# Both mixers of the first block worked out between the projection units, and two banks for the modulation rows

## The reference, cut to what matters

```python
def hybrid_mixer(h, positions, w_in, w_alpha, b_alpha, gla_g, gn_g, gn_b, w_out):
    proj = (h @ w_in).astype(F32)                      # 256 tokens, 1024 -> 3600
    gq, gk, gv, gr, ga, rq, rk, rv, rg = jnp.split(proj, np.cumsum(IN_SPLITS)[:-1], axis=-1)
    log_a = jax.nn.log_sigmoid(ga @ w_alpha + b_alpha) / GLA_TAU
    o_g = gla_core(...)                                # 4 heads, chunks of 64, states passed on
    o_g = o_g * lax.rsqrt(jnp.mean(o_g * o_g, axis=-1, keepdims=True) + EPS)
    o_g = o_g.reshape(bsz, seq, GLA_V) * gla_g * jax.nn.silu(gr)
    rq, rk = rotary(rq) * RET_DK ** -0.5, rotary(rk)
    o_r = retention_core(rq, rk, rv, log_gamma)        # 4 heads, chunks of 64
    mu = jnp.mean(o_r, axis=-1, keepdims=True)
    var = jnp.mean(jnp.square(o_r - mu), axis=-1, keepdims=True)
    o_r = ((o_r - mu) * lax.rsqrt(var + EPS) * gn_g + gn_b) * jax.nn.silu(rg)
    return jnp.concatenate([o_g, o_r], axis=-1) @ w_out

mod = (silu(c) @ ada_w[layer] + ada_b[layer])          # 6 x 1024 values: shift, scale, gate
h = rms_norm(x, g) * (1.0 + sc1) + sh1
x = x + g1 * hybrid_mixer(h, ...)
```

## Time and profile before

| | us |
|---|---|
| median of three runs | 3511.22 |
| profiled execution, its own time | 3509.48 |
| its span | 3507.7 |
| PE busy | 3230.5 (92%) |
| DVE busy | 1596.4 (46%) |
| ACT busy | 1308.8 (37%) |
| mean granted PE clock | 0.946 |

### The profile page before, as it was taken

One profiled execution on the slowest core, in us unless ns is written; L12 is line 12 of the kernel. 1 busy time (PEld: TensorE's weight loads), 2 busy tenths in 40 slices (PEclk: granted clock), 3 DMA queues, 4 the chain that ended last, 5 costly groups with the idle time before them and its releaser, 6 DMA issues.

```text
span 3507.7 us, 53042 instructions
## 1 busy us (share of the span) xinstructions
PE 3230.5 (92%) x20598; PEld 2784.8 (79%) x20598; DVE 1596.4 (46%) x2304; ACT 1308.8 (37%) x1930; POOL 0.2 (0%) x4
## 2 busy tenths in 40 slices
PE   7878998769999999998999998999999999988899
PEld 5767888669999999996776776778777777776798
DVE  4544445445555555553232345533234232346454
ACT  4334334324444444444222244432223222244444
POOL 0000000000000000000000000000000000000000
PEclk9979999769999999999999998999999999998999
DMA  9627673216666666664535321144443535521354
GB/s 319 202 77 233 203 236 124 72 49 197 199 190 190 188 191 192 196 180 115 180 90 164 122 74 49 49 123 128 125 129 92 170 117 144 162 80 65 107 167 137
DMA packets 668224, 511.02 MB, mean 146 GB/s; under 512 B 14411, under 2 KB 662030, under 8 KB 667926
## 3 DMA queue, kind: packets, MB, share of 16 engines
q1 hardware_dynamic: 588838, 390.55, 38.2%
q10 hardware_dynamic: 79216, 118.01, 10.7%
HBM read 507.46 MB, written 1.05 MB: 145 GB/s over the span
## 4 chain that ended last, share of the span: by engine, by line
PE 86%; ACT 5%; DVE 5%; DMA 2%; issue 1%; SPq 1%; ACTq 0%; DVEq 0%
PE bank L595 26%; PE bank L596 25%; PE bank L597 25%; PE bank L623 3%; ACT ring L1158 2%; DMA ada_halves<-in_ada_w 1%; PE bank L1047 1%; PE bank L630 1%; PE bank L1056 1%; PE bank L1068 1%; ACT hn_split L1157 1%; PE bank L835 1%; ACT hn_split L1165 1%; DVE weights_split L1483 1%; ACT weights_split L1104 1%
## 5 line engine op out<-in xcount | busy, mean ns | idle before, releaser
L595 PE MATMUL bank<-hn_split,weights_split 128*128 128x256 f32 (+1 forms) x4016 | 1319.1, 328 | 104.5 <-DVE hn_split L1529 30.3
L596 PE MATMUL bank<-hn_split,weights_split 128*128 128x256 f32 (+1 forms) x4016 | 1292.5, 322 | 0.0
L597 PE MATMUL bank<-hn_split,weights_split 128*128 128x256 f32 (+1 forms) x4016 | 1291.0, 321 | 0.0
L1104 ACT ACTIVATE weights_split<-weights_raw 128x1024 fp32r<-128x1024 f32 (+2 forms) x670 | 748.4, 1118 | 652.8 <-PE bank L597 634.1
L595 PEld LDWEIGHTS bank<-hn_split,weights_split 128*128 128x128 f32 x4016 | 784.6, 195 | 256.7 <-issue 124.9
L1483 DVE TENSOR_TENSOR weights_split<-weights_raw,weights_split 128x1024 fp32r<-128x1024 f32 (+2 forms) x670 | 873.3, 1304 | 245.1 <-ACT weights_split L1104 241.1
L597 PEld LDWEIGHTS bank<-hn_split,weights_split 128*128 128x128 f32 x4016 | 784.5, 195 | 53.0
L596 PEld LDWEIGHTS bank<-hn_split,weights_split 128*128 128x128 f32 x4016 | 785.9, 196 | 49.1 <-issue 1.0
L1569 DVE TENSOR_TENSOR ring<-ring,bank 128x256 f32<-128x256 f32 (+1 forms) x198 | 101.1, 511 | 1010.7 <-PE bank L597 923.1
L595 PE MATMUL bank<-hidden_split,weights_split 128*128 128x256 f32 (+1 forms) x1584 | 507.8, 321 | 0.0
L596 PE MATMUL bank<-hidden_split,weights_split 128*128 128x256 f32 (+1 forms) x1584 | 504.4, 318 | 0.0
(11 more groups left out here) (279 smaller groups left out, 1839.7 us busy)
## 6 DMA issues: line engine op xcount, KB each, us to landing
weights_raw<-in_moe_w SPq DMA_DIRECT2D x176, 512.0 KB, 5.2
weights_raw<-in_w_ffn_in SPq DMA_DIRECT2D x176, 512.0 KB, 5.1
ada_halves<-in_w_ada ACTq DMA_DIRECT2D x96, 768.0 KB, 4.8
weights_raw<-in_w_in SPq DMA_DIRECT2D x84, 512.0 KB, 4.8
ada_halves<-in_ada_w ACTq DMA_DIRECT2D x54, 768.0 KB, 5.1
weights_raw<-in_moe_w SPq DMA_DIRECT2D x32, 768.0 KB, 4.5
weights_raw<-in_w_ffn_out SPq DMA_DIRECT2D x32, 768.0 KB, 4.6
weights_raw<-in_ffn_w SPq DMA_DIRECT2D x44, 512.0 KB, 5.5
```

The costliest lines, as they stand in the source:

```text
L595: mm(ps, wh, xh, start=first, stop=False)
L596: mm(ps, wh, xl, start=False, stop=False)
L597: return mm(ps, wl, xh, start=False, stop=last)
L1104: act.activation(split_view(slot, 0, kts, n), raw, ACT.Copy).then_inc(split_high, 1)
```

## The change

The units of the input projection come in another order: the gates of both mixers last (retention 21 to 24, GLA 25 to 28), the values in 13 to 20. The whole retention work moves between units, and the GLA updates and outputs go behind it. The norms of the mixer outputs are no longer summed and rooted over 1024 columns: squares are summed into 8 columns (`sums`, a table row `tokpick` with a single column of ones, now 15 wide, picks the place), ACT takes the root of 8 columns, DVE the reciprocal of 8 and a diagonal matrix (`rstd_diagonal`), and PE spreads it (`spread`). The mixers' split outputs have buffers of their own (`MIXG`, `MIXR`), so `out1` no longer uses `hn`; it runs its first two units together, the retention tiles first, then one GLA tile after the other. The residual reads banks 0 and 1 there. In layer 0 the angle work (13 DVE instructions) moves from behind unit 2 to behind unit 9. In the feed-forwards the rows of a chunk go to bank 7 or 6 in turn.

PE at the end of layer 1's input projection, before: the end of the retention outputs, then the means and squares, then the output projection (names: `ret_out` the mixer output, `out_squares` its squares, `hn_split` the split input of a product).

```diff
--- before.py
+++ after.py
...
         OR, _ = at("ret_out", 1024, [P, 4, SEQ], F32, g_at + 9472)
-        SR2, _ = at("ret_state", 1536, [P, 3, 4, P], F32, hn_at + 2048)
+        SR2 = [at(f"ret_state{i}", 512, [P, 4, P], F32, g_at + w)[0] for i, w in enumerate((2048, 2560, 10496))]
+        MIXG, _ = at("gla_split", 2048, [P, 2, 4, SEQ], F32R, g_at)
+        MIXR, _ = at("ret_split", 2048, [P, 2, 4, SEQ], F32R, g_at + 3072)
         SQO, _ = at("out_squares", 1024, [P, 1024], F32, ring_at)
-        RTO, _ = at("out_rstd", 1024, [P, 1024], F32, ring_at + 1024)
...
+
+        U_GA, U_GQ, U_GK, U_RQ, U_RK, U_RV, U_GV, U_RG, U_GG = 2, 0, 3, 5, 9, 13, 17, 21, 25
         for layer in range(DEPTH):
             w = a["w_in"][layer]
             phase(f"in1.{layer}")
-            for c in (0, 256):
-                load(w, c, 256, KT, HALVES)
+            load(w, 0, 256, KT, HALVES)
             load(w, 1536, P, KT, ((0, P),))
-            load_rows(w, 512)
-            for c in (1024, 1280) + tuple(1552 + 256 * i for i in range(4)):
+            for c in (256,) + tuple(1552 + 256 * i for i in range(4)):
                 load(w, c, 256, KT, HALVES)
             load_rows(w, 2576)
-            for c in (3088, 3344):
+            load_rows(w, 512)
+            for c in (3088, 3344, 1024, 1280):
                 load(w, c, 256, KT, HALVES)
             phase(f"out1.{layer}")
             for c in range(0, D, 256):
...
-                            pe.wait_ge(ada_copied, x.chunk(g, c))
-                        ada_half_rows(7, condp, h)
+                            pe.wait_ge(ada_copied, x.chunk(g, c - (x.per > 1)))
+                        ada_half_rows(7 - c % 2, condp, h)
                     if h == 1 and p == at_unit + 3:
                         if c == 0:
                             pe.wait_ge(mod_ready, g + x.mods)
...
+            def out1(name, layer):
+
+                u0, _ = PH[name]
+                order = (4, 5, 6, 7, 0, 1, 2, 3)
+                part = lambda k, p: (MIXG, MIXR)[k // 4][:, p, k % 4, :]
+
+                def products(m, k):
+                    w = [split_view((u0 + m) % 3, p, KT, P)[:, k, :] for p in (0, 1)]
+                    i = passes(PS[m % 2][:, 0:SEQ], w, [part(k, p) for p in (0, 1)], k == order[0], k == order[-1])
+                    if k == order[-1]:
+                        i.then_inc(unit_done, 1)
+
+                pe.wait_ge(split_both, u0 + 2)
+                for k in order:
+                    pe.wait_ge(S["mixed"], 5 * layer + (1 if k >= 4 else k + 2))
+                    for m in (0, 1):
+                        products(m, k)
+                for m in range(2, KT):
+                    pe.wait_ge(x_updated, XU[name] + m - 1)
+                    pe.wait_ge(split_both, u0 + m + 1)
+                    for k in order:
+                        products(m, k)
...
 
                     pe.wait_ge(S["gla_keys_copied"], layer + 1)
-                    pe.wait_ge(S["gla_selected"], 8 * (layer + 1))
-                    posted(7)
-                    posted(8)
...
+                def sums(ready, place, signal):
+
                     pe.wait_ge(*ready)
+                    for b in range(8):
+                        x = mm(PS[4][:, place:place + 8], SQO[:, b * P:(b + 1) * P], tab("tokpick")[:, 7 - b:15 - b],
+                               start=b == 0, stop=b == 7)
+                    x.then_inc(signal, 1)
+
+                def spread(diagonal, signal):
                     for j in range(2):
-                        x = mm(PS[5 + j][:, :], tab("ones"), rhs[:, j * 512:(j + 1) * 512], start=True, stop=True)
+                        pe.wait_ge(diagonal, 2 * layer + j + 1)
+                        x = mm(PS[5 + j][:, :], tab("ones"), RTO[:, 4 * j:4 * j + 4, :].rearrange("p a b -> p (a b)"),
+                               start=True, stop=True)
...
+                extra = {4: alpha, 9: gla_scores, 11: lambda: rope_turn(RQ, U_RQ, 2, "rope_q_turned"),
+                         14: lambda: rope_turn(RK, U_RK, 5, "rope_k_turned"), 16: ret_scores, 18: ret_updates,
...
-                ret_outputs()
-                sums((S["ret_copied"], layer + 1), OR[:, :, :].rearrange("p a b -> p (a b)"), S["ret_means"])
-                sums((S["ret_squares"], layer + 1), SQO, S["ret_sums"])
-                pe.wait_ge(S["mixed"], 2 * (layer + 1))
-                out_phase(f"out1.{layer}", T)
+                posted(27)
+                posted(28)
+                out1(f"out1.{layer}", layer)
                 norm(f"out1.{layer}", T)
                 wait_h()
...
                         act.wait_ge(ada_used, x.halves(g, c, 1) + 2)
                         act.wait_ge(ada_done, x.done(g, c - 1))
-                        act.activation(AROW[:, :], PS[7][:, 0:ADA_COLS], ACT.Copy).then_inc(ada_copied, 1)
+                        act.activation(AROW[:, :], PS[7 - c % 2][:, 0:ADA_COLS], ACT.Copy).then_inc(ada_copied, 1)
 
             def out_phase(name):
...
+                def gla_copy():
+                    for h in range(HEADS):
+                        c = (h // 2) * SEQ
+                        x = act.activation(OG[:, h, :], PS[2 + h % 2][:, c:c + SEQ], ACT.Copy, scale=col("gla_norm_g", 4 * layer + h))
+                    x.then_inc(S["gla_copied"], 1)
+                    roots((S["gla_sums"], layer + 1), 448, 32, S["gla_roots"])
+
+                def roots(ready, place, at_col, signal):
                     act.wait_ge(*ready)
-                    for j in range(2):
-                        x = act.activation(RTO[:, j * 512:(j + 1) * 512], PS[5 + j][:, :], ACT.Sqrt, bias=tab("eps"),
-                                           scale=1.0 / P)
...
+                extra = {5: gate_log, 7: decay_exp, 10: gla_keys, 11: trig, 17: ret_keys, 20: ret_copy, 22: ret_squares,
+                         23: lambda: roots((S["ret_sums"], layer + 1), 440, 16, S["ret_roots"]), 25: gla_squares,
...
                     dve.wait_ge(unit_done, u + 1)
                     for s in range(seg):
-                        residual(m, s, PS[2 + m % 2][:, s * 256:s * 256 + 256], gate(m, s))
+                        residual(m, s, PS[(0 if name[:4] == "out1" else 2) + m % 2][:, s * 256:s * 256 + 256], gate(m, s))
                 dve.wait_ge(x_updated, XU[name] + KT * seg)
 
...
+                def rstd_diagonal(roots, at_col, diagonal):
+                    dve.wait_ge(roots, layer + 1)
+                    link(dve.reciprocal(SMALL[:, at_col + 8:at_col + 16], SMALL[:, at_col:at_col + 8]))
+                    for j in range(2):
+                        r = SMALL[:, at_col + 8 + 4 * j:at_col + 12 + 4 * j]
+                        tt(RTO[:, 4 * j:4 * j + 4, :], tab("ident").unsqueeze(1).broadcast_to([P, 4, P]),
+                           r.unsqueeze(2).broadcast_to([P, 4, P]), ALU.mult).then_inc(diagonal, 1)
+
                 def gla_scale():
-                    dve.wait_ge(S["gla_roots"], layer + 1)
-                    link(dve.reciprocal(RTO[:, :], RTO[:, :]))
+                    dve.wait_ge(S["gla_copied"], layer + 1)
                     for h in range(HEADS):
-                        c = (h // 2) * SEQ
-                        tt(OG[:, h, :], PS[2 + h % 2][:, c:c + SEQ], RTO[:, (h % 2) * 512 + c:(h % 2) * 512 + c + SEQ],
-                           ALU.mult).then_inc(S["gla_scaled"], 1)
-                    dve.wait_ge(S["gla_scaled"], 4 * (layer + 1))
-                    posted(11)
-                    posted(12)
+                        posted(U_GG + h)
+                        tt(OG[:, h, :], OG[:, h, :], RG_G[:, h, :], ALU.mult).then_inc(S["gla_scaled"], 1)
+                    dve.wait_ge(S["gla_spread"], layer + 1)
+                    for h in range(HEADS + 1):
+                        if h < HEADS:
+                            dve.wait_ge(S["gla_scaled"], 4 * layer + h + 1)
+                            c = (h // 2) * SEQ
+                            tt(OG[:, h, :], OG[:, h, :], PS[5 + h % 2][:, c:c + SEQ], ALU.mult).then_inc(S["gla_weighted"], 1)
+                        if h >= 1:
+                            dve.wait_ge(S["gla_high"], 4 * layer + h)
+                            tt(MIXG[:, 1, h - 1, :], OG[:, h - 1, :], MIXG[:, 0, h - 1, :].bitcast(F32), ALU.subtract)\
+                                .then_inc(S["mixed"], 1)
+
...
+                extra = {5: gate_abs, 6: decay, 8: gla_products, 10: gla_select,
+                         12: lambda: rope(RQ, 2, (S["rope_q_turned"], layer + 1), S["rope_q_made"]),
...
                         dve.wait_ge(unit_done, u0 + i + 1)
-                        src = ps[0:16, 0:SEQ] if i == 4 else ps[:, 0:SEQ]
+                        src = ps[0:16, 0:SEQ] if i == U_GA else ps[:, 0:SEQ]
                         dve.tensor_copy(dst, src).then_inc(drained[i % 2], 1)
```

More of the change, by code:

```diff
@@ new lines, in ret_copy, with ret_squares @@
+                def ret_copy():
+                    act.wait_ge(S["ret_outputs"], layer + 1)
+                    for j in range(2):
```

(6 more changed lines are left out.)

233 lines of the change are left out of this document (116 added, 117 removed).

## The result

| | before | after |
|---|---|---|
| median of the runs, us | 3510.8 (4 runs) | 3420.03 (4 runs, 3418.57 to 3423.51) |
| ratio, 95% interval | | 0.9743 (0.9726 to 0.976) |
| profiled execution, us (its span) | 3509.48 (3507.7) | 3419.33 (3416.4) |
| mean granted clock of TensorE | 0.946 | 0.966 |

The kernel is 2.6% faster. The forecast was 3417 us. Its total is right within 3 us, but by luck: two of its terms were too small and a third was missing, and they nearly cancel. The rest of this document is about that.

What follows compares the result with a forecast made beforehand. TensorE was taken as the bound, losing time only when idle or at its lower clock. Savings of 34.5 (layer 1), 28.5 (layer 0) and 31.3 (banks), 94.3 us, took 3509.5 to 3415.2, plus 1.7 for the median: 3417, range 3394 to 3452.

Steps and rivals of the forecast that it cites:

- first block and what moves with it: Both layers' stretch from third projection unit to norm: 34.5 us saved in layer 1 and 28.5 in layer 0.
- two row banks: Modulation rows in the feed-forwards: 28.1 us saved with 512 tokens, 3.2 of 6.4 with 256; sum 31.3, ends 0 and 34.5.
- The tail: Behind the last projection unit: retention now lies between units, leaving 1.4 us of wait where 14.2 was.
- the second rival's exposed chain: Late GLA root puts diagonal, spread, gate and split behind unit 28: 8.2 us per layer, 3433 us; chance 0.12.
- The waits: New TensorE waits between units and at the end: 9.9 plus 3.2 us in layer 1, 12.0 in layer 0.
- The small products: Mixer norms: eight 8-column products at 1.6 us and a spread at 1.9 replace two sums, adding 3.2 per layer.
- The clock: Both layers' blocks: 3 us lost in each of two output stretches and 2 for one wait, 8 per layer.
- 132.5: Layer 1, third unit through output projection: TensorE's work in us at the upper clock level, before the change.
- 158.7: Layer 0's same stretch: TensorE's work in us, with half chunks, extra turns and context turns added.
- Rows' waits back: First rival, feed-forwards: halves' DMA or ACT's queue eats what the second bank frees; 31.3 us return, 3448 us; chance 0.10.
- Clock down at every wait: Third rival: nine waits or small-product runs per layer cost 3 us each, 38 more in all, 3455 us; chance 0.12.
- The fourth: Rival: clock stays low from unit 9 to the output projection's end in both layers, 3634 us; chance 0.03.

Runs made afterwards that it cites:

- one bank, code placed: The aligned kernel with the modulation rows back in one bank, so the first block's part of the change alone: 3428.21 us, ratio 0.9778.
- banks alone: The kernel before with only the two row banks added, its first block left as before: 3469.24 us, ratio 0.9884.
- aligned: The changed kernel with 60 more TensorE instructions (repeated waits) ahead of layer 1's router, moving the expert loop's start: 3389.03 us, ratio 0.9662.
- the kernel with the outputs halved: The aligned kernel with the GLA outputs cut in two, heads 0 and 1 behind unit 24, 2 and 3 behind 25: 3383.68 us, ratio 0.9646.

## Why the prediction was right, and where it was not

The total is a sum of three terms, each with an error:

| term | forecast, us | measured, us | from |
|---|---|---|---|
| first block and what moves with it | -63.0 | -82 | one bank, code placed, against before |
| of it, third unit to norm in both layers | -63.0 | -70.7 | rows of after against the earlier trace rows |
| two row banks | -31.3 | -39 to -40 | banks alone; one bank against aligned |
| place of the expert loop's code | none | +31 | after against aligned |
| sum (the second row is part of the first) | -94.3 | -90.8 | medians, after against before |

*The tail.* Right. Its two waits went, no wait over 2 us stands between unit 28 and the norm (1.3 and 0.7 us at most), and the second rival's exposed chain did not come.

*The waits, the step of the block's sum that failed.* In layer 1, from the third unit on, 13.1 us were forecast and 9.3 came (153.99 less 144.69): the 3.0, 3.0, 1.2, 0.4 and 1.4 as 2.95, 2.65, 1.23, 0.56 and 1.27, but nothing ahead of unit 9 (1.7) and only 0.62 of the 1.8 at the third unit. In layer 0 12.0 were forecast and 7.1 came: 4.2 and 1.3 for the row copy were 3.94 and 1.19, the third wait and the late half chunk (3.3) did not come. That is 8.7 us less; PE's busy time took 0.9 more than my work and clock together, and so both layers beat the forecast by 7.7. My chain took each late split as a wait and let the units behind a wait run at full speed. They ran slower (7.65 us for units 8 and 9, 5.99 at full clock), and that covered the wait of unit 9: in the kernel with the outputs halved, where they did not, it was there with 1.38 us.

*The small products.* Eight were priced at 1.6 and the spread at 1.9. From the first of each to the next work it is 1.71 and 1.32:

```profile
604.48:606.19 1.71, 1.71 (x19) 1.00 0.00 0
623.56:624.88 1.32, 1.32 (x6) 1.00 0.06 12
```

*The clock.* About right in size, wrong in place. With my 132.5 and 3.2 of work, layer 1 had 9.0 us of it and layer 0 7.9 (169.82 less 161.9), where 8 each was forecast. But that is a remainder, and it takes in every error of the work. By the granted clock, layer 1 ran 17.1 us at the lower level and layer 0 10.2, which costs half of it: 8.5 and 5.1 us, 13.6 in place of 16. So 2.8 us of layer 0's remainder are work that my 158.7 left out. And 3 of the 8 were charged to the retention outputs, since their length at 0.50 was all that the earlier trace rows showed; between dense units they ran at 1.00 in both layers. The GLA outputs with the unit behind them cost 4.5 in layer 1 and 3.1 in layer 0 (9.59 and 8.89 for what takes 6.9 at full clock, and 4.83 and 4.12 for a unit of 2.97). In layer 1 the two early waits add 1.7 in units 8 and 9, which only took the place of unit 9's wait, and 1.6 in the scores; in layer 0 the wait of 3.94 us adds 1.7.

*The banks, mis-sized.* The mechanism was right: all waits on the copy went, and the DMA waits on the halves rose from 12.1 us over the whole span to 18.1 with the banks alone (17.5 in the changed kernel), which is nearly all of the 6.4 that left the 256-token phase; I had half of it coming back, and that phase gained nothing. The 512-token phases gained more than their 28.1 us of waits, 43.1 with the banks alone and 37.7 in the changed kernel's setting, because the term held waits only. The removed waits (16 there, the longest 2.5 us) also gave back clock: by PE's busy time 7.0 us in the first such phase and 8.0 in the second with the banks alone, 2.9 and 6.2 in the other setting.

*The step that was missing.* No term and no rival held the place of code in a loop that the change does not touch. It is as large as the banks' term was forecast, with the opposite sign, and it hid the two underestimates. That the range held the time is luck: without the loop's shift the time is 3389 (the aligned kernel), below the low end of 3394. (The two steps that lead to that end, 12 and 9 us, give 3396.)

*The rivals.* Rows' waits back (3448): true in the 256-token phase, false in the others. Exposed chain (3433): false. Clock down at every wait (3455), the one that the Trainium skill's "TensorE: Matmul & The Clock Gate", section "HAM oscillation — how this bites in real kernels", speaks for: false within units, where waits of 1.2 and 0.6 us left the clock at 1.00. The page's loop waits 3 to 5 us each time; the one wait of that length in these stretches, 3.94 us for layer 0's row copy, was followed by the lower level (0.62 over the next 4.0 us). Waits of 2.5 to 3 us went both ways. The 2.65 us wait ahead of the scores put them at the lower level here, as the 2.30 us one had the earlier trace rows: from their start to the end of the 32 records (3.7 us, against 2.1 in the kernel with the outputs halved, where the clock stayed at 1.00 behind the same wait).

```profile
75.85:79.85 4.00, 4.00 (x23) 0.62 0.67 199
540.97:544.66 3.69, 3.69 (x32) 0.54 0.33 114
```

The fourth (3634): false, the clock was 0.94 and 0.97 in the two stretches.

## What to carry to other kernels

When a change adds or removes instructions ahead of a long loop, look at the packets of the instruction queue and at "issue" waits in the loop before judging the change: the same edit can gain or lose 1% by where the loop begins, and a few dozen instructions in a place where the engine waits anyway put it right. When a wait is priced, add the clock it costs: here a third to a half as much again in the dense phases. But where another engine's chain sets when the next work can start, slower products only shorten the next wait. And a total that comes out right is no evidence for its parts; only the runs with one part each showed three errors that cancel.

## What the runs showed of the hardware

- A TensorE loop of 1697 instructions (8 turns) cost 31 to 36 us more in one place of the code than in the others; the instruction queue moved 185 packets in place of 130 to 132. That it then lies across 8 blocks of 256 instructions and not 7 is worked out from five starts.
- A repeated wait on a semaphore long reached costs TensorE's issue 0.1 us per instruction (5.3 us for 60, 12.0 for 122), and nothing was seen of 60 of them in a place where TensorE waited 9 us anyway.
- The retention outputs ran at full clock between dense units (4.62 us in the row above); the same 40 records behind the last unit took 8.71 at the lower level, in the kernel before.
- The GLA outputs (40 records, the state's products on 64 rows) lost the clock in each of 20 stretches of 7 us of work, and in 1 of 12 of 3.5 us.
- The same wait of 2.95 us between dense units was followed by the lower clock in five kernels and not in two; with a wait of 3.94 us in layer 0 it fell in all nine kernels that have it.
